# Unused products of 256 bf16 columns between the tiny products of the two compressions, in a two-layer decoder trunk

## The chip, the cores and the metric

The kernel runs on one core of a Trainium2 chip. The metric is the device time of one execution in microseconds (us), from the first to the last instruction and what lies around them. TensorE (PE) has a clock that the chip grants at one of two levels, 2.4 GHz (1.00 in the profile) and 1.2 GHz (0.50).

## The reference, cut to what matters

Two decoder layers on 256 tokens of width 1024. Each layer has one input projection, four parallel mixers (latent attention, a three-branch sparse attention called NSA, a gated linear recurrence, a state-space mixer), an output projection and a feed-forward part; the first layer's is dense, the second's is a mixture of 8 experts. All is float32.

The change lies in NSA's compression: keys and values of 64 dimensions are cut into 15 overlapping blocks of 32 tokens, and each block is multiplied by a weight of 32·64 by 64.

```python
def compress(t, pe, w):
    ch = t.reshape(B, S // CMP_STRIDE, CMP_STRIDE, d)
    blk = jnp.concatenate([ch[:, :-1], ch[:, 1:]], axis=2)
    return ((blk + pe).reshape(B, nc, CMP_LEN * d) @ w).astype(F32)

kc = compress(keys[:, :, 0], cmp_pe[0], w_cmp[0])
vc = compress(vals[:, :, 0], cmp_pe[1], w_cmp[1])
```

with `S` 256, `CMP_STRIDE` 16, `CMP_LEN` 32, `d` 64 and `nc` 15. The results `kc` and `vc` (15 by 64) are the keys and values of the "compressed" attention branch.

## The kernel before, in words

Each engine has its own program, and semaphores tie them together. SyncE (SP) loads weights in units of 1 MB into a ring of seven slots. ScalarE (ACT) copies each unit to a rounded part `w_hi` (L1259 in the mixers, L1281 for the experts), VectorE (DVE) takes the rest as `w_lo` (L1693, L1714), and TensorE makes three one-pass products of each (L450 to L452, and L578, L581 in `by_channel`). These large products fill the feed-forward parts and the input and output projections.

A mixer stage of a layer is written out by hand as TensorE's order: the input projections, then a loop over eight attention jobs `AJ` (MLA, selected, window, compressed; two token blocks each, n = 0 to 7). In step n TensorE does `scores(n)` (a bias product of 512 bf16 columns, L671, that writes the mask, and q·k products, L679), `products(n-2)` (probabilities by values, L713), and `turn_probs(n-1)` (transposes of probabilities, which are products with the identity matrix, L694). Between them stand the other mixers' small products, in this order:

- n = 1: `scores(1)`, `compressed_keys`, `turn_probs(0)`;
- n = 2: `scores(2)`, `products(0)`, `turn_probs(1)`, `compressed_values`;
- n = 3: `scores(3)`, `products(1)`, `turn_probs(2)`, `lru_square` (L800);
- n = 4: `scores(4)`, `products(2)`, `turn_probs(3)`, `ssd_sums` (L754 to L769);
- n = 5 to 7: the same three of each job, `ssd_cb` (L779), `ssd_products` (L789, L792), and the first part of the output projection.

`compressed_keys` (L723) is 32 float32 products that accumulate in one PSUM bank: 64 rows of the array, 64 columns of weights, 15 moving columns each. `compressed_values` (L731) is 32 with 64 rows, 15 columns of weights and 64 moving columns. The trace records each float32 product twice ("x64" for 32), each record with a weight load of its own.

PSUM has eight banks in two pools of four. `bank(0)` hands out the next bank of pool 0 and makes TensorE wait until the reader of its last contents (ACT's exponentials at L1431, DVE's sum at L1924, DVE's copies `kcT` at L1997 and `vc` at L2005) has taken them; `give` says which engine reads it next.

During this stage DVE also runs the recurrence's scan and the state-space mixer's convolutions (L1988 to L1992, L1792, L1795), and ACT the activations that follow (L1474, L1475). The transposes of the normed residual are at L430.

Of the kernel before, what the change touches and what calls it, by code (L numbers as in the profile page):

```python
# [23 lines left out]
P = 128  # L24
# [16 lines left out]
def trunk(nc, x, positions, norm_mix, w_in, mla_q_norm, mla_w_uq, mla_kv_norm, mla_w_ukv, nsa_cmp_pe,  # L41
# [33 lines left out]
    with ctx:  # L75
        def sb(name, shape, dt=F32):
            return ctx.enter_context(nc.sbuf_tensor(name, shape, dt))
# [10 lines left out]
        ident_b = sb("ident_b", [P, P], BF16)  # L88
        cbias = sb("cbias", [P, 2 * P], BF16)
# [299 lines left out]
        def _(pe):  # L389
# [3 lines left out]
            def claim(k):  # L393

                if free_after[k] is not None:
                    pe.wait_ge(*free_after[k])

            def bank(pool):

                k = 4 * pool + used_banks[pool] % 4  # L400
                used_banks[pool] += 1
                claim(k)
                return banks[k]
# [8 lines left out]
            def give(mm, who, b):  # L412

                given[who] += 1
                s = (for_dve, for_act)[who]
                mm.then_inc(s, 1)
                taken(who, b, s, given[who])
# [21 lines left out]
            b = bank(0)  # L439
# [96 lines left out]
            for l in range(L):  # L536
# [162 lines left out]
                def products(n):  # L699
# [15 lines left out]
                    give(mm, 0, b)  # L715
                    mark["pv", l, n] = gave[0]

                def compressed_keys():

                    pe.wait_ge(cin_ready, l + 1)  # L720
                    b = bank(0)
                    for j in range(CLEN):
                        mm = pe.matmul(b[0:HD, 0:NC], w_cmp[0:HD, j, :], cin[0:HD, j, :], start=(j == 0),  # L723
                                       stop=(j == CLEN - 1))
                    give(mm, 0, b)

                def compressed_values():

                    b = bank(0)
                    for j in range(CLEN):  # L730
                        mm = pe.matmul(b[0:NC, 0:HD], cin[HD:P, j, :], w_cmp[HD:P, j, :], start=(j == 0),  # L731
                                       stop=(j == CLEN - 1))
                    give(mm, 0, b)
                    mark["cmp", l] = gave[0]
# [112 lines left out]
                for n in range(1, len(AJ)):  # L847
                    scores(n)
                    if n >= 2:
                        products(n - 2)  # L850
                    if n == 1:
                        compressed_keys()
                    turn_probs(n - 1, 0 if n == 7 else 1)
                    if n == 2:
                        compressed_values()
                    if n == 3:
                        lru_square()
                    if n == 4:
                        ssd_sums()
                    if n == 5:  # L860
                        ssd_cb()
                    if n == 6:
                        ssd_products()
                    if n == 7:
                        turn_output(0)
                        project_output(0)
# [1414 lines left out]
```

## Time and profile before

| what | value |
|---|---|
| runs of the kernel | 1625.79, 1629.19, 1631.63 us; median 1629.19 us |
| profiled execution, its own time | 1629.23 us |
| its span in the profile | 1627.4 us |
| mean granted clock of TensorE | 0.951 |
| PE busy | 1546.0 us, 95% of the span |
| DVE busy | 1229.1 us, 76% |
| ACT busy | 1017.4 us, 63% |
| chain of work that ended last | PE 93%, DVE 3%, issue 2%, ACT 1% |

The profiled execution's time is 1.8 us over its span. "Busy" counts the time in which at least one instruction of the engine is under way. A start time of a row is in us from the span's start; the time that a group of PE instructions holds the engine is best read as the distance to the start of the next one, since the recorded duration of a product includes its way through the array. Layer 0's mixer stage ends near 181 us, layer 1's runs from about 440 to 611 us.

### The profile page before, as it was taken

How to read it: one execution, taken by the hardware profiler on the slowest of the kernel's cores; microseconds unless marked ns; L12 is line 12 of the kernel's file. 1: busy time of each engine (PE TensorE's matmuls, PEld its weight loads, DVE VectorE, ACT ScalarE, POOL GpSimd, SP SyncE). 2: the span in 40 equal slices, each digit the busy share in tenths (PEclk: the TensorE clock that was granted, in tenths of full speed). 3: DMA queues.
4: the chain of work that ended last, by engine and by line, in shares of the span. 5: the costliest groups of instructions: out<-in, count | busy, mean ns of one | idle time of the engine just before them, and what ended most of it. 6: DMA issues, size and time to landing. Idle time of an engine off the chain costs nothing.

```text
span 1627.4 us, 20283 instructions
## 1 busy us (share of the span) xinstructions
PE 1546.0 (95%) x7476; PEld 1292.2 (79%) x7476; DVE 1229.1 (76%) x1150; ACT 1017.4 (63%) x941; POOL 81.8 (5%) x110
## 2 busy tenths in 40 slices
PE   7998799999799984999999999999999999999996
PEld 6887688888689864888888888888888888888884
DVE  6747544444567455888989988988988988988985
ACT  5645343444345522778778778778778778777763
POOL 2100000000000001000000000000000000000000
PEclk9968999999898685999999999999999999999998
DMA  9521555555330052999999999999999999999991
GB/s 288 136 61 60 205 187 198 184 181 192 103 118 1 27 181 78 358 395 358 376 394 356 382 393 352 388 393 344 395 394 343 394 396 342 393 397 352 394 397 43
DMA packets 189878, 444.67 MB, mean 273 GB/s; under 512 B 9633, under 2 KB 15918, under 8 KB 189822
## 3 DMA queue, kind: packets, MB, share of 16 engines
q1 hardware_dynamic: 185214, 427.82, 71.6%
q0 software_dynamic: 4608, 16.10, 3.9%
q8 instruction: 35, 0.57, 0.1%
q14 instruction: 21, 0.17, 0.0%
HBM read 436.03 MB, written 7.86 MB: 273 GB/s over the span
## 4 chain that ended last, share of the span: by engine, by line
PE 93%; DVE 3%; issue 2%; ACT 1%; DMA 0%; POOL 0%; SPq 0%; ACTq 0%; DVEq 0%; POOLq 0%
PE bank L451 25%; PE bank L452 25%; PE bank L450 25%; PE bank L578 3%; PE bank L713 2%; PE bank L505 2%; PE bank L679 2%; PE bank L581 1%; PE bank L694 1%; PE bank L731 1%; PE bank L723 1%; DVE hT L1669 1%; PE bank L915 0%; PE bank L430 0%; DVE w_lo L1693 0%
## 5 line engine op out<-in xcount | busy, mean ns | idle before, releaser
L1714 DVE TENSOR_TENSOR w_lo<-ring,w_hi 128x2048 fp32r<-128x2048 f32 x375 | 853.4, 2290 | 193.3 <-ACT w_hi L1281 192.6
L1281 ACT ACTIVATE w_hi<-ring 128x2048 fp32r<-128x2048 f32 x375 | 716.1, 1915 | 221.6 <-PE bank L450 221.5
L451 PE MATMUL bank<-w_hi,xT_hi 128*128 128x512 f32 x896 | 354.4, 396 | 5.8 <-ACT w_hi L1281 5.8
L452 PE MATMUL bank<-w_hi,xT_lo 128*128 128x512 f32 x896 | 350.4, 391 | 0.0
L450 PE MATMUL bank<-w_lo,xT_hi 128*128 128x512 f32 x896 | 240.4, 390 | 0.0
L451 PE MATMUL bank<-w_hi,hidT_hi 128*128 128x512 f32 x560 | 220.5, 394 | 1.6 <-DVE hidT_lo L1721 1.6
L452 PE MATMUL bank<-w_hi,hidT_lo 128*128 128x512 f32 x560 | 218.3, 390 | 0.0
L451 PEld LDWEIGHTS bank<-w_hi,xT_hi 128*128 128x128 f32 x896 | 168.8, 188 | 40.1 <-ACT w_hi L1281 6.2
L450 PEld LDWEIGHTS bank<-w_lo,xT_hi 128*128 128x128 f32 x896 | 168.7, 188 | 35.7
L452 PEld LDWEIGHTS bank<-w_hi,xT_lo 128*128 128x128 f32 x896 | 169.0, 189 | 33.9
L451 PE MATMUL bank<-w_hi,hT_hi 128*128 128x512 f32 (+2 forms) x384 | 150.3, 395 | 7.9 <-DVE hT_lo L1955 4.5
L450 PE MATMUL bank<-w_lo,hidT_hi 128*128 128x512 f32 x560 | 147.8, 389 | 0.0
L452 PE MATMUL bank<-w_hi,hT_lo 128*128 128x512 f32 (+2 forms) x384 | 147.7, 388 | 0.0
L451 PEld LDWEIGHTS bank<-w_hi,hidT_hi 128*128 128x128 f32 x560 | 105.2, 188 | 23.1 <-DVE hidT_lo L1721 1.8
L450 PEld LDWEIGHTS bank<-w_lo,hidT_hi 128*128 128x128 f32 x560 | 105.1, 188 | 22.2
L452 PEld LDWEIGHTS bank<-w_hi,hidT_lo 128*128 128x128 f32 x560 | 105.2, 188 | 21.3
L1287 ACT ACTIVATE hidT_hi<-bank 128x512 fp32r<-128x512 f32 x70 | 41.2, 599 | 105.0 <-PE bank L505 105.0
L451 PEld LDWEIGHTS bank<-w_hi,hT_hi 128*128 128x128 f32 x384 | 74.6, 194 | 22.8 <-DVE hT_lo L1955 5.0
L450 PE MATMUL bank<-w_lo,hT_hi 128*128 128x512 f32 (+2 forms) x384 | 91.7, 380 | 0.0
L1693 DVE TENSOR_TENSOR w_lo<-ring,w_hi 128x2048 fp32r<-128x2048 f32 (+1 forms) x31 | 70.5, 2282 | 26.3 <-ACT w_hi L1259 25.8
L452 PEld LDWEIGHTS bank<-w_hi,hT_lo 128*128 128x128 f32 x384 | 74.4, 194 | 13.7
L450 PEld LDWEIGHTS bank<-w_lo,hT_hi 128*128 128x128 f32 x384 | 70.2, 188 | 13.6
(344 smaller groups left out, 1380.8 us busy)
## 6 DMA issues: line engine op xcount, KB each, us to landing
ring<-in_moe_w_gate_dram SPq DMA_DIRECT2D x112, 1024.0 KB, 10.0
ring<-in_moe_w_up_dram SPq DMA_DIRECT2D x112, 1024.0 KB, 9.4
ring<-in_moe_w_down_dram SPq DMA_DIRECT2D x112, 1024.0 KB, 9.5
ring<-in_ffn_w_gate_dram SPq DMA_DIRECT2D x14, 1024.0 KB, 5.1
ring<-in_ffn_w_up_dram SPq DMA_DIRECT2D x14, 1024.0 KB, 5.1
ring<-in_ffn_w_down_dram SPq DMA_DIRECT2D x14, 1024.0 KB, 4.8
ring<-in_w_in_dram SPq DMA_DIRECT2D x12, 1024.0 KB, 5.3
ring<-in_w_out_dram SPq DMA_DIRECT2D x8, 1024.0 KB, 5.0
```

What stands on the lines that cost most here:

```text
L450: return pe.matmul(o, x_hi, w, start=False, stop=stop)
L451: pe.matmul(o, x_hi, w, start=start, stop=False)
L452: return pe.matmul(o, x_lo, w, start=False, stop=False)
L505: mm = pe.transpose(banks[2 + v][:, f * P:(f + 1) * P], hid[:, v, f * P:(f + 1) * P], ident[:, :])
L578: mm = pe.matmul(o, wk, hT_hi[:, 4 * h + k, :], start=start and not low, stop=stop and low)
L581: pe.matmul(o, wk, hT_lo[:, 4 * h + k, :], start=False, stop=False)
L679: mm = pe.matmul(b[:, i * nk:(i + 1) * nk], q, k, start=False, stop=(i == per - 1))
L713: mm = pe.matmul(b[:, h * HD:(h + 1) * HD], probT[0:rows, n % 2, i * P:(i + 1) * P], v, start=(kb == 0), stop=(kb == nb - 1))
L1281: act.activation(w_hi[:, (base + at) % SPLIT, :], ring[:, i, :], ACT.Copy).then_inc(hi_ready, 1)
L1287: act.activation(hidT_hi[:, v, :], banks[2 + v][:, :], ACT.Copy).then_inc(hidT_hi_ready, 1)
L1693: dve.tensor_tensor(dst[:, :, 0:n], slot_k(p)[:, :, 0:n], hi[:, :, 0:n], ALU.subtract)\
L1714: dve.tensor_tensor(w_lo[:, v, :], ring[:, (base + at) % RING, :], w_hi[:, v, :].bitcast(F32), ALU.subtract).then_inc(lo_ready, 1)
```

## The change

A helper `stay_warm` issues one product of the 128 x 128 bf16 identity with the 256 bf16 columns of `cbias` (a mask constant) into a spare PSUM bank whose contents nobody reads. Before every second product of both compressions it is called, so 16 times in `compressed_keys` and 16 times in `compressed_values`, in both layers: 64 such products in all. The spare bank is taken from pool 0 with `bank(0)` and never given to a reader.

```diff
+                def stay_warm(b):
+
+                    pe.matmul(b[:, 0:2 * P], ident_b[:, :], cbias[:, :], start=True, stop=True)
+
                 def compressed_keys():
 
                     pe.wait_ge(cin_ready, l + 1)
                     b = bank(0)
+                    spare = bank(0)
                     for j in range(CLEN):
+                        if j % 2 == 0:
+                            stay_warm(spare)
                         mm = pe.matmul(b[0:HD, 0:NC], w_cmp[0:HD, j, :], cin[0:HD, j, :], start=(j == 0),
                                        stop=(j == CLEN - 1))
                     give(mm, 0, b)
@@ -727,7 +734,10 @@
                 def compressed_values():
 
                     b = bank(0)
+                    spare = bank(0)
                     for j in range(CLEN):
+                        if j % 2 == 0:
+                            stay_warm(spare)
                         mm = pe.matmul(b[0:NC, 0:HD], cin[HD:P, j, :], w_cmp[HD:P, j, :], start=(j == 0),
                                        stop=(j == CLEN - 1))
                     give(mm, 0, b)
```

## Rows read from the trace of the kernel before

**Rows 1.** The page's 40 slices of the span: TensorE's granted clock, in tenths.

```profile
PEclk9968999999898685999999999999999999999998
```

**Rows 2.** Stretches from:to in us: length, busy us (xcount) by engine, granted clock, DMA share, GB/s.

```profile
89.64:91.88 2.24, 2.24 (x40) 2.24 (x39) 2.07 (x4) 1.41 (x7) 0.00 (x0) 1.00 0.00 0
91.88:119.20 27.32, 27.32 (x155) 23.18 (x154) 12.54 (x29) 11.56 (x29) 3.43 (x4) 0.50 0.30 60
...
139.70:146.50 6.80, 6.30 (x28) 5.74 (x28) 5.82 (x11) 2.00 (x10) 0.00 (x0) 0.50 0.27 73
...
518.54:556.09 37.55, 37.55 (x184) 32.30 (x184) 17.52 (x41) 17.83 (x42) 0.00 (x0) 0.50 0.09 29
```

**Rows 3.** Timeline of PE in layer 0: start us, busy us, line, tiles, shape, count.

```profile
87.37 0.39 PE L671 MATMUL bank<-cbias,ident_b 128*128 128x512 bf16 x1
87.60 1.03 PE L679 MATMUL bank<-work 96*128 96x256 f32 x4
...
89.64 5.17 PE L723 MATMUL bank<-ring,w_cmp 64*64 64x15 f32 x64
94.74 1.11 PE L694 MATMUL bank<-ident,ring 128*128 128x128 f32 x4
...
101.81 7.00 PE L731 MATMUL bank<-w_cmp,ring 64*15 64x64 f32 x64
108.75 0.61 PE L671 MATMUL bank<-cbias,ident_b 128*128 128x512 bf16 x1
```

**Rows 4.** Timeline of PE in layer 0, behind the return to the full clock.

```profile
119.53 0.38 PE L671 MATMUL bank<-cbias,ident_b 128*128 128x512 bf16 x1
119.84 1.16 PE L679 MATMUL bank<-work 64*128 64x128 f32 x8
120.92 1.10 PE L713 MATMUL bank<-work,ring 128*128 128x64 f32 x8
121.86 1.05 PE L694 MATMUL bank<-ident,ring 128*128 128x128 f32 x8
122.75 0.60 PE L754 MATMUL bank<-ident,work 128*128 128x128 f32 x4
...
126.84 1.13 PE L679 MATMUL bank<-work 64*128 64x256 f32 x4
127.90 0.39 PE L671 MATMUL bank<-cbias,ident_b 128*128 128x512 bf16 x1
```

**Rows 5.** Timeline of PE in layer 1, the same stage.

```profile
514.68 3.90 PE L723 MATMUL bank<-ring,w_cmp 64*64 64x15 f32 x64
518.52 1.11 PE L694 MATMUL bank<-ident,ring 128*128 128x128 f32 x4
...
541.93 1.91 PE L800 MATMUL bank<-hn,ones 128*128 128x256 f32 x4
543.64 0.63 PE L671 MATMUL bank<-cbias,ident_b 128*128 128x512 bf16 x1
...
549.67 1.06 PE L754 MATMUL bank<-ident,work 128*128 128x128 f32 x4
```

**Rows 6.** Waits of PE from 86 to 150 us: us in total, times, longest.

```profile
PE bank L694 <- issue: 0.5, 1, 0.5
```

**Rows 7.** Timeline of DVE and of ACT in layer 0.

```profile
97.27 0.17 DVE L1997 COPY kcT<-bank 64x15 f32<-64x15 f32 x1
```

```profile
106.16 0.61 ACT L1475 ACTIVATE work<-work 128x512 f32<-128x512 f32 x1
```

**Rows 8.** Behind the mixer stage: transposes on PE, and the stretch after them.

```profile
183.82 1.74 PE L430 MATMUL bank<-ident,hn 128*128 128x128 f32 x8 [2.45 <-DVE hn L1660]
185.95 1.80 PE L430 MATMUL bank<-ident,hn 128*128 128x128 f32 x8 [0.40 <-DVE hn L1660]
```

```profile
183.80:187.50 3.70, 3.29 (x16) 2.90 (x16) 1.47 (x3) 2.09 (x4) 0.81 (x2) 0.54 0.00 0
187.50:190.90 3.40, 0.26 (x2) 0.01 (x1) 3.30 (x6) 2.51 (x5) 0.00 (x0) 0.99 0.01 2
```

## The prediction

> **What bounds the kernel now.** The first view is the page: the chain that ended last is 93% PE, and PE is busy 95% of the span. What shortens PE's own stream where nobody else is late shortens the kernel. The second is the clock by slices [rows 1]: it is 9 tenths nearly everywhere but drops to 6 to 8 tenths in a few slices, among them the third (81 to 122 us) and the thirteenth to fifteenth (488 to 610 us), where the mixers run. The third is the stretches [rows 2]: in layer 0 the clock falls to 1.2 GHz at 91.88 us and stays there for 27.32 us; in layer 1 it falls at 518.54 and stays for 37.55 us. PE is busy without a break in both (27.32 of 27.32, 37.55 of 37.55), and its waits over 86 to 150 us add up to 0.5 us [rows 6]. So the engine is not starved there; it does dense work at half rate, and it alone is the path. The fourth view is the timeline [rows 3, 5]: what PE did before each fall is the block of 32 key products of 15 moving columns. In layer 0 it had run 2.24 us of it, in layer 1 all 3.84 us. Before that block the clock was 1.00. After the fall it does not come back through the other attention work, though the same kinds of work at full clock keep it later on (119.5 to 139.7 us).
>
> **The change part by part.** It removes nothing. It adds 16 unused products to each compression of each layer, 64 in all, and one claimed bank to each.
>
> *If the clock stays at 2.4 GHz, the old work gets shorter.* I price every piece between the end of the key block and `ssd_sums` at full clock, by the distance from start to start. From rows 4: a bias product 0.31 (119.53 to 119.84), eight score records of 128 columns 1.08, eight L713 records 0.94, eight transposes 0.89 (so four 0.445), and four score records of 256 columns 1.06 (126.84 to 127.90). `lru_square` has no row fully at 2.4 GHz; at 1.2 it takes 1.71 (541.93 to 543.64 [rows 5]), half is 0.855. The values' 64 records are also seen at 1.2 GHz alone, 6.94 us (101.81 to 108.75 [rows 3]). Half, 3.47, is the lower bound, 6.94 the upper; the key block's 64 records at 2.4 GHz take 3.84 (514.68 to 518.52), and being as many loads and products it is the nearest row, so I take 3.84.
> In order: turn_probs(0) 0.445, scores(2) 1.39, products(0) 0.94, turn_probs(1) 0.89, values 3.84, scores(3) 2 x 1.37 = 2.74, products(1) 1.88, turn_probs(2) 0.445, lru_square 0.855, scores(4) 1.39, products(2) 0.94, turn_probs(3) 0.89. Sum 16.65 us.
> Layer 0 takes 28.01 us for this (94.74 to 122.75 [rows 3, 4]): 11.36 saved. Its key block takes 5.10 (89.64 to 94.74) against 3.84: 1.26 more. Together 12.62.
> Layer 1 takes 31.15 us (518.52 to 549.67 [rows 5]): 14.50 saved. Its `ssd_sums` then runs at half clock until 556.09, 6.42 us, of which half, 3.21, is saved. Together 17.71. Both layers: 30.3 us.
>
> *The unused products themselves.* No row shows one of 256 columns. The bf16 product of 512 columns holds PE 0.23 us in a full stream (87.37 to 87.60 [rows 3]), so its half is 0.115. Below: a weight load of the next tiny product can hide behind it, and a tiny record is 0.06 (3.84 / 64), which leaves 0.06. Above: the same bias product takes 0.31 where the kind of product changes around it, which is 0.08 more, so 0.20. I take 0.12, since the tiny records around it are bound by their loads and part of the switch is hidden. 64 x 0.12 = 7.7 us; bounds 3.8 and 12.8.
>
> *The spare bank.* `bank(0)` makes PE wait for the bank's last reader. In the key block it is the bank of scores(0), whose exponentials are over before the block begins. In the value block it is the same bank again, which no reader was given since. Every later claim in pool 0 then falls on the bank two further on: scores(2) on that of scores(1), values on that of the keys (`kcT`, copied at 97.27 [rows 7]), and from lru_square on each claim again meets the bank of the same earlier job as now. No wait; below nothing is excluded, as nothing is taken away, and above it is some tenths. If one is late it is DVE's `kcT`, because DVE reaches it by its own chain of convolutions; the key block with its products ends at 89.64 + 3.84 + 1.9 = 95.4, the values start at 95.4 + 3.67 = 99.1, 1.6 us behind the copy.
>
> *Other engines at the faster pace.* The cover for everything above is that DVE and ACT keep up. DVE is free of its convolutions at 97.6, and scores(2) now ends at 97.2, so that sum is 0.4 late with nobody behind it until products(2). ACT's L1475 ends at 106.8 [rows 7], and lru_square is reached at 99.1 + 5.76 + 2.74 + 1.88 + 0.445 = 109.9: 3 us of slack. These two follow from work that does not depend on PE's pace. Weight transfers use 0.30 and 0.09 of the DMA engines in the two stretches [rows 2], and those of the later units are released by DVE and ACT steps that move forward with PE. SP's and POOL's queues get nothing new. I price this at 0, up to 2 us if the slack is misjudged.
>
> The sum: 30.3 - 7.7 = 22.6 us off the profiled execution's own 1629.23 us, which is the median of the runs (1629.19): **1606.6 us**. With the bounds of the product's cost it is 1602.7 to 1611.7, and the values' price can add 0.7 off or, far less likely, more on.
>
> **A rule against the change.** PE was busy for all of both stretches, and the clock fell nonetheless [rows 2]. The Trainium skill, TensorE: Matmul & The Clock Gate, section Why this matters for your kernels, says that drops come from PE-idle gaps between bursts of matmuls; taken alone that says there is no gap here to fill, and the products would only be a cost; its outcome is rival B below. The rows speak against it, as the clock fell with no gap at all.
>
> **The rivals.**
> *B, the clock falls in the blocks as before (slower).* Each pair of tiny products is four records at 0.06, 0.24 us, against one unused product of about 0.12 us: the block is still mostly tiny work. If the clock falls about where it does now, everything behind it stays as it is and the unused products come on top: per layer 8 at 0.12 and 24 at the price of the slow clock. That is half of the bias product's 0.54 to 0.57 there, or some 0.25. 8 x 0.12 + 24 x 0.25 = 7.0 us, twice 14: 1643 us. It decides in the key block, the leaner of the two. For it: nothing in the trace shows such a mixture. Against it: scores on 64 rows and products of 64 columns keep 1.00 from 119.5 to 135.9 without a single dense block.
> *C, the clock is held in both blocks and falls behind the values.* There, transposes and small products stand with nothing between them. Then layer 0 gains 1.26, 7.07 - 3.67 = 3.40 up to the values and 3.10 in them, layer 1 the last two: 14.3 - 7.7 = 6.6, so 1622.6 us. The rows speak for the opposite: 16 transposes, and nothing else, ran from 183.82 to 187.7, and the clock rose from 0.5 to 1.00 during them [rows 8]. The Trainium skill, TensorE: Matmul & The Clock Gate, section Part 4: PE-mode transpose, states that a transpose does not count as PE-busy in the same way; by that rule C would be likely. By the trace it is not.
> *D, the clock is held in one layer only.* Where the fall lands differs between the layers now (2.24 and at least 3.84 us into the same block), so chance plays a part. Layer 1 alone: 17.7 - 3.8 - 7.0 = 6.9 off, 1622; layer 0 alone: 12.6 - 3.8 - 7.0 = 1.8 off, 1627.
>
> **How the numbers follow.** Forecast 0.70, B 0.10, C 0.10, D 0.10. Two of the forecast's uncertainties are left: the later half-clock stretches of 6.80 us (139.70, and one like it in layer 1 [rows 2]) can shift by a few us, each worth up to 3.4 us, and runs of one kernel spread by 5.8 us. So the forecast's own range is 1600 to 1613. Reaching to C and to the better case of D gives **1600 to 1623** with 0.84 inside it. About 0.3%, 4.9 us, is what can be told from no change. Faster by more: forecast, C and half of D, 0.84, rounded to 0.83. Within: the other half of D and a B softened by a clock that comes back sooner, 0.06. Slower: the rest of B, with its 14 us, 0.11.
>
> **What would show it.** Right: the granted clock reads 1.00 from the key block to about 137 us (layer 0) and about 555 us (layer 1); the key block and the value block take some 5.8 us each; from the key block to `ssd_sums` PE needs 16.65 + 3.84 + 3.8 = 24.3 us instead of 33.1 and 35.0; the mean clock rises from 0.951 to about 0.97; PE's waits in the stage stay under 1 us. Wrong: a fall inside the key block (B), a fall behind the values with the blocks at full clock (C), idle time of PE at L679, L713 or L694 that DVE or ACT releases (misjudged cover), or blocks longer than 6.5 us at full clock (mis-sized product).

## The result, and the profile after

The change makes the kernel slower: 1646.02 us median (1644.32 to 1650.57, four runs) against 1630.03 us for the kernel before, a ratio of 1.0107 with a 95% interval of 1.0078 to 1.0135. Forecast was 1606.6 us, range 1600 to 1623. The profiled execution took 1645.25 us (span 1643.4), 16.0 more than the one of before.

The page's slices of the granted clock after the change, in tenths, beside [rows 1]:

```profile
PEclk9988899999898686899999999999999999999998
```

The third slice is better than before (8 for 6) and the sixteenth too (6 for 5), but the fifth and the seventeenth are 8 now where they were 9, and the fourteenth, in layer 1's mixers, is 6 as before. The mean clock is 0.952 against 0.951: nothing was won on the whole, and the products came on top.

Stretches of the changed kernel (from:to, length, busy by engine, granted clock, DMA share, GB/s), beside [rows 2]:

```profile
90.17:95.79 5.62, 5.62 (x52) 4.00 (x50) 5.17 (x9) 1.98 (x9) 0.00 (x0) 1.00 0.00 0
95.85:109.36 13.51, 13.51 (x69) 10.34 (x68) 5.84 (x16) 4.66 (x13) 0.00 (x0) 0.50 0.01 2
109.40:143.60 34.20, 34.20 (x265) 27.36 (x265) 20.01 (x46) 23.76 (x60) 4.40 (x6) 1.00 0.35 79
...
518.45:522.40 3.95, 3.95 (x37) 2.80 (x35) 3.61 (x6) 1.98 (x9) 0.00 (x0) 1.00 0.02 6
522.45:563.36 40.91, 40.91 (x193) 27.34 (x193) 11.55 (x29) 12.62 (x27) 0.00 (x0) 0.50 0.05 16
563.40:583.80 20.40, 20.40 (x161) 18.46 (x160) 16.44 (x35) 15.95 (x45) 0.95 (x2) 1.00 0.05 20
```

The clock falls inside the key block of both layers, 5.6 us into it in layer 0 and 4.0 us into it in layer 1 (before: 2.2 us into it, and at its end). It comes back after 13.5 us in layer 0, inside the value block, and only after 40.9 us in layer 1 (before: 27.3 and 37.6).

The timeline of PE in the changed kernel: one group of the key block at the full clock, one at half, the work behind, and groups of the value block. L720 is the unused product, L730 the keys, L741 the values.

```profile
90.71 0.28 PE L720 MATMUL bank<-cbias,ident_b 128*128 128x256 bf16 x1
90.92 0.40 PE L730 MATMUL bank<-ring,w_cmp 64*64 64x15 f32 x4
91.26 0.28 PE L720 MATMUL bank<-cbias,ident_b 128*128 128x256 bf16 x1
...
99.86 0.40 PE L720 MATMUL bank<-cbias,ident_b 128*128 128x256 bf16 x1
100.19 0.61 PE L730 MATMUL bank<-ring,w_cmp 64*64 64x15 f32 x4
100.72 1.11 PE L694 MATMUL bank<-ident,ring 128*128 128x128 f32 x4
...
107.66 0.42 PE L720 MATMUL bank<-cbias,ident_b 128*128 128x256 bf16 x1
...
112.10 0.28 PE L720 MATMUL bank<-cbias,ident_b 128*128 128x256 bf16 x1
112.32 0.39 PE L741 MATMUL bank<-w_cmp,ring 64*15 64x64 f32 x4
112.64 0.28 PE L720 MATMUL bank<-cbias,ident_b 128*128 128x256 bf16 x1
...
116.95 0.39 PE L671 MATMUL bank<-cbias,ident_b 128*128 128x512 bf16 x1
...
126.07 0.60 PE L764 MATMUL bank<-ident,work 128*128 128x128 f32 x4
```

A group of one unused product and four tiny records takes 0.55 us at the full clock (90.71 to 91.26), where four tiny records alone take 0.24. So an unused product adds **0.31 us, not 0.12**. At half clock a group takes about 0.87 us (99.86 to 100.72). Four tiny records alone take about 0.43 there: 64 of the value block take 6.94 [rows 3]. So the product adds 0.44. In the value block at the full clock it is 0.54 (112.10 to 112.64).

Where the time went in us, stage by stage, from the start times of both traces:

| stretch | layer 0 before | after | layer 1 before | after |
|---|---|---|---|---|
| key block | 5.10 | 10.55 | 3.84 | 11.50 |
| turn_probs(0) to the values | 7.07 | 6.94 | 7.07 | 6.94 |
| value block | 6.94 | 9.29 | 6.94 | 13.79 |
| scores(3) to `ssd_sums` | 14.00 | 9.12 | 17.14 | 15.07 |
| `ssd_sums` | 3.78 | 3.78 | 6.86 | 3.78 |
| sum of differences | | +2.8 | | +9.2 |

The two blocks cost 7.8 us more in layer 0 and 14.5 in layer 1; the clock that comes back gives 4.9 back in layer 0 and 5.2 in layer 1. Between the blocks another 0.3 comes back. Together that is 12.0 of the 16.0 us. The other 4 lie in stages that the change doesn't touch (0.5 before the first key block, 2.0 between and behind the two stretches up to the last products, 1.4 at the end), which is within the 5.8 us by which runs of one kernel differ.

### The profile page after: what moved, and what is told of

The parts are those of the page before. It is cut to its first block, busy times and chain, and to the rows that moved or that the text cites. A ratio compares the mean times of both kernels' runs of the same rounds, so it can differ in the third digit from the quotient of the medians.

```text
span 1643.4 us, 20413 instructions
## 1 busy us (share of the span) xinstructions
PE 1560.0 (95%) x7540; PEld 1289.9 (78%) x7540; DVE 1229.3 (75%) x1150; ACT 1017.5 (62%) x941; POOL 81.9 (5%) x110
## 4 chain that ended last, share of the span: by engine, by line
PE 92%; DVE 4%; issue 2%; ACT 1%; POOL 1%; DMA 0%; POOLq 0%; ACTq 0%; DVEq 0%
PE bank L451 25%; PE bank L452 25%; PE bank L450 25%; PE bank L578 2%; PE bank L505 2%; PE bank L713 2%; PE bank L679 1%; PE bank L581 1%; PE bank L720 1%; PE bank L741 1%; PE bank L730 1%; PE bank L694 1%; DVE hT L1679 1%; PE bank L925 0%; PE bank L430 0%
```

## The experiments

Each is written against the changed kernel. "Before" medians on the same chips were 1630.3 to 1631.5 us.

### e1: the same 64 products, but together in the middle of each block

```diff
                     for j in range(CLEN):
-                        if j % 2 == 0:
-                            stay_warm(spare)
+                        if j == CLEN // 2:
+                            for _ in range(16):
+                                stay_warm(spare)
```

(in both blocks)

> The same 64 unused products, but the 16 of each block stand together in its middle instead of before every second tiny product. Theory S (each unused product between tiny ones pays for two changes of the kind of product, about 0.2 us, in which nothing streams; so the block is long and thin and the clock falls): one pair of changes per block is left, a block takes 3.84 + 16 x 0.115 + 0.2 = 5.9 us at full clock, the granted clock stays 1.00 from the key block to about 137 us and in layer 1 likewise; time about 1630.0 - 30.3 + 8.2 = 1608 us. Rival H (the tiny products pull the clock down whatever stands between them, the arrangement does not matter): the clock falls in the key block again and the time stays at 1640 to 1650 us.

Measured: 1617.56 us median (1615.04 to 1623.72), ratio 0.9928 with an interval of 0.9901 to 0.9954. PE in layer 0:

```profile
89.92 2.03 PE L731 MATMUL bank<-ring,w_cmp 64*64 64x15 f32 x32
91.88 1.92 PE L720 MATMUL bank<-cbias,ident_b 128*128 128x256 bf16 x16
93.73 2.03 PE L731 MATMUL bank<-ring,w_cmp 64*64 64x15 f32 x32
95.70 0.66 PE L694 MATMUL bank<-ident,ring 128*128 128x128 f32 x4
...
114.24 0.60 PE L766 MATMUL bank<-ident,work 128*128 128x128 f32 x4
```

and its stretches in both layers:

```profile
95.70:133.00 37.30, 37.30 (x316) 32.45 (x314) 26.96 (x60) 28.21 (x72) 4.38 (x6) 1.00 0.32 73
507.98:515.40 7.42, 7.42 (x93) 6.68 (x93) 6.93 (x13) 2.82 (x10) 0.00 (x0) 1.00 0.02 3
515.45:525.60 10.15, 10.15 (x64) 8.65 (x63) 5.39 (x14) 6.16 (x14) 0.00 (x0) 0.50 0.01 2
```

Sixteen unused products in a row take 1.85 us (91.88 to 93.73), 0.116 each, which is what the prediction worked out for one in a full stream. The key block takes 5.78 us instead of 10.55. In layer 0 the clock holds throughout, and the way from the key block to `ssd_sums` is 24.32 us (89.92 to 114.24). In layer 1 it holds in the block but falls 1.6 us behind it, at 515.4, for 10.2 us. So the number and kind of the products is the same as in the change, and the arrangement alone is worth 28 us. Rival H falls. Layer 1's loss of the clock behind the block explains half of the 10 us by which the time lies above the expectation: from the key block to `ssd_sums` it took 29.12 us (507.98 to 537.10), 4.8 more than layer 0.

### e2: as e1, in the key block only

```diff
-                    spare = bank(0)
                     for j in range(CLEN):
-                        if j % 2 == 0:
-                            stay_warm(spare)
                         mm = pe.matmul(b[0:NC, 0:HD], cin[HD:P, j, :], w_cmp[HD:P, j, :], start=(j == 0),
```

(and e1's edit in `compressed_keys`)

> As e1, but with the 16 products in the key block only; the value block is as in the kernel before. Theory S: the value block, with 64 moving columns in each product, holds the full clock by itself once it begins at it, and the time is about 1630.0 - 30.3 + 4.1 = 1604 us. Rival V (the value block loses the clock when nothing stands in it): the clock is 1.00 up to the value block and falls inside or behind it; the gain is then only the one before the values, 1.3 + 3.4 in layer 0 and 3.4 in layer 1, less 4.1: about 1626 us.

Measured: 1619.23 us median (1617.29 to 1629.63), ratio 0.995, interval 0.9921 to 0.998. The traced run has both outcomes, one in each layer:

```profile
89.57:129.30 39.73, 39.73 (x367) 34.92 (x366) 30.95 (x69) 30.14 (x80) 4.38 (x6) 1.00 0.30 69
...
511.80:535.50 23.70, 23.70 (x123) 19.29 (x122) 8.29 (x22) 11.74 (x26) 0.00 (x0) 0.50 0.09 26
```

In layer 0 the value block, with nothing in it, holds the full clock, so rival V falls there: no unused product is needed among the values. In layer 1 the clock falls at 511.7, again right behind the key block (which ends at 510.18), this time for 23.9 us. Both falls, of e1 and e2, point to the second half of the key block and the work right behind it as the weak place; e5 tries that.

### e3 and e4: what makes an unused product cost 0.31 us

e3 puts it on 64 rows (`r0`, given by the caller, is 0 in the key block and 64 in the value block), e4 in float32 on 128 rows:

```diff
-                    pe.matmul(b[:, 0:2 * P], ident_b[:, :], cbias[:, :], start=True, stop=True)
+                    pe.matmul(b[:, 0:2 * P], ident_b[r0:r0 + HD, :], cbias[r0:r0 + HD, :], start=True, stop=True)
```

```diff
-                    pe.matmul(b[:, 0:2 * P], ident_b[:, :], cbias[:, :], start=True, stop=True)
+                    pe.matmul(b[:, 0:HD], ident[:, :], ident[:, 0:HD], start=True, stop=True)
```

> The change, with each unused product on 64 rows of the array (the same rows as the tiny products around it) instead of 128, still bf16 and 256 columns. Theory S in the form that the change between a 128-row and a 64-row product is what costs: a group of one unused and four tiny records takes 0.24 + 0.12 = 0.36 us at full clock, against 0.546 now. Rival T (the change between bf16 and float32 is what costs): it stays at 0.52 to 0.55 us. Either way the clock still falls in the key block, so the time stays within 1632 to 1650 us.

> The change, with each unused product in float32 (identity by 64 of its columns, two records of about 0.12 us) on 128 rows. Theory S (rows): the group takes 0.24 + 0.24 + 0.2 = 0.68 us at full clock, since the change of rows is still there. Rival T (type): 0.48 us. The clock falls in the key block in both; time 1640 to 1660 us.

One run each: 1655.28 and 1669.53 us, both above what was expected (1650 and 1660 at most). e3 and then e4, PE at the full clock:

```profile
90.28 0.28 PE L720 MATMUL bank<-cbias,ident_b 64*128 64x256 bf16 x1
90.49 0.40 PE L730 MATMUL bank<-ring,w_cmp 64*64 64x15 f32 x4
90.83 0.28 PE L720 MATMUL bank<-cbias,ident_b 64*128 64x256 bf16 x1
```

```profile
91.30 0.43 PE L720 MATMUL bank<-ident 128*128 128x64 f32 x2
91.66 0.40 PE L730 MATMUL bank<-ring,w_cmp 64*64 64x15 f32 x4
91.99 0.32 PE L720 MATMUL bank<-ident 128*128 128x64 f32 x1
```

The group stays at 0.55 us with equal rows (90.28 to 90.83), so the change of rows is not needed for the cost: the form of theory S written for e3 falls. It takes 0.69 us with equal type (91.30 to 91.99), as S said for e4 (0.68) and not T (0.48), so the type is not it either. In both, the unused product still has 128 columns of weights where the tiny ones have 64.

### e6: the unused product on the same tile as its neighbours

```diff
-                    pe.matmul(b[:, 0:2 * P], ident_b[:, :], cbias[:, :], start=True, stop=True)
+                    n = HD if r0 == 0 else NC
+                    pe.matmul(b[0:n, 0:2 * P], ident_b[r0:r0 + HD, 0:n], cbias[r0:r0 + HD, :], start=True, stop=True)
```

> The change, with each unused product on the same tile of the array as the tiny products around it (64 x 64 in the key block, 64 x 15 in the value block), still bf16 and 256 columns. Theory S (the change of tile, rows or columns, costs about 0.2 us per pair, because the next weights are not loaded ahead): a group of one unused and four tiny records takes about 0.36 us at full clock instead of 0.546. Rival T (the change between bf16 and float32 costs it): still 0.52 to 0.55 us. The clock may fall in both.

One run: 1627.68 us. PE in the key block:

```profile
90.70 0.27 PE L721 MATMUL bank<-cbias,ident_b 64*64 64x256 bf16 x1
90.82 0.35 PE L731 MATMUL bank<-ring,w_cmp 64*64 64x15 f32 x4
91.02 0.27 PE L721 MATMUL bank<-cbias,ident_b 64*64 64x256 bf16 x1
```

0.32 us for a group, 0.08 more than the tiny records alone. The type still changes twice in it, so rival T falls. **What costs is the change of tile**: 0.55 against 0.32, 0.23 us for a pair of changes. By e3 a change of columns is enough; that a change of rows alone costs too is seen only in the scores of the kernel before (below). The weight loads show where the time goes. In the changed kernel (PEld, first fence) the tiny products' first load begins 0.21 us after the unused product (90.71 to 90.92); on the same tile (second fence) the next load begins 0.03 us after the last one:

```profile
90.71 0.10 PEld L720 LDWEIGHTS bank<-cbias,ident_b 128*128 128x128 bf16 x1
90.92 0.30 PEld L730 LDWEIGHTS bank<-ring,w_cmp 64*64 64x64 f32 x4
```

```profile
90.67 0.11 PEld L721 LDWEIGHTS bank<-cbias,ident_b 64*64 64x64 bf16 x1
90.70 0.36 PEld L731 LDWEIGHTS bank<-ring,w_cmp 64*64 64x64 f32 x4
```

The Trainium skill, TensorEngine Tiling (Array Packing), section Key Properties, has this rule: changing the tiling mode drains the engine. The traces agree and give the price of 0.23 us, for which the prediction should have looked.

The clock fell in e6 too, in the key block of layer 0 at 93.8 and of layer 1 at 517.1, 3.4 and 4.1 us into it, and came back in layer 0's value block at 104.1. So taking the changes of tile out of the interleaved block did not hold the clock. But this filler differs from that of the change in a second point, as it uses a quarter of the array; no run has full-size filler between the tiny products without changes of tile.

### e7 and e8: one block of the change at a time

e7 leaves the value block as before, e8 the key block (each takes the three added lines out of the other function).

> The change's unused products in the key block only, between the tiny products as in the change; the value block as in the kernel before. The key block of the changed kernel takes 10.6 us in layer 0 and 11.5 in layer 1, against 5.1 and 3.8 before. Theory S: the block still loses the clock and nothing brings it back sooner than before: 1630.5 + 5.5 + 7.7, about 1643 us. Rival R (the rest of the stage profits from the dense work ahead of it): under 1635 us.

> The change's unused products in the value block only; the key block as before, so the clock falls in it. In the changed kernel the clock came back inside layer 0's value block (109.4 us) and not in layer 1's. Theory S: a value block at half clock takes 13.8 us instead of 6.9, and 9.3 where the clock comes back in it, which then saves some 9 us of what follows; so between 1630.5 - 2 x 6 = 1618 us (both come back) and 1630.5 + 2 x 6.9 = 1644 us (neither); with one of each about 1631 us. Rival R2 (the return in layer 0 had nothing to do with the unused products): 1640 to 1645 us in every run.

e7: 1642.62 us median (1640.34 to 1643.92), ratio 1.006, interval 1.0038 to 1.0082, as theory S had it. The clock falls about 4 us into both key blocks and stays down for 34 us (94.6 to 128.7, 528.1 to 562.2).

e8: 1644.35 us median of ten, ratio 1.0061 with an interval of 1.0034 to 1.0087, but the ten fall into three groups: 1622.23 once; 1632.89, 1633.14, 1633.26; and six from 1644.24 to 1650.34. These are about the three values worked out beforehand for "the clock comes back in both value blocks, in one, in neither" (1618, 1631, 1644). The traced run is the 1622.23, and in it the clock is back in both:

```profile
91.90:101.90 10.00, 10.00 (x57) 8.75 (x56) 7.62 (x18) 3.71 (x14) 0.00 (x0) 0.50 0.00 1
102.10:139.50 37.40, 36.35 (x284) 29.06 (x282) 23.53 (x52) 24.97 (x61) 4.39 (x6) 1.00 0.32 73
518.60:525.20 6.60, 6.60 (x29) 5.37 (x27) 5.83 (x15) 3.18 (x12) 0.00 (x0) 0.50 0.00 0
525.40:562.70 37.30, 36.32 (x284) 29.02 (x282) 23.46 (x51) 24.96 (x61) 0.95 (x2) 1.00 0.09 29
```

So the clock comes back, and then stays at 1.00, in value blocks in which unused products and tiny ones alternate at 0.54 us a group, two changes of tile in each (102.1 to 110.4 in layer 0). Whether a half-clock block is left early differs from run to run of one program. That the other two groups are "one" and "neither" is inferred from their times and from their mean granted clocks: 0.961 in the traced run, 0.954 to 0.955 in the group about 1633, 0.944 to 0.948 in the six.

### e9: four products in the middle instead of sixteen

```diff
-                        if j % 2 == 0:
-                            stay_warm(spare)
+                        if j == CLEN // 2:
+                            for _ in range(4):
+                                stay_warm(spare)
```

(key block; none in the value block)

> As e2, but with 4 unused products in the middle of the key block instead of 16. Theory S (how much dense work stands between the tiny products decides): 4 are too few, the clock falls in or behind the block in both layers as in the kernel before, and 2 x 0.7 us come on top: 1630 to 1634 us, the granted clock at 0.50 for some 27 us or more in each layer. Rival Q (a break of any length in the run of tiny products is enough): the clock holds as with 16, 1602 to 1619 us.

Measured: 1632.18 us median of ten (1628.1 to 1639.57), ratio 1.002, interval 0.9998 to 1.0041. The clock falls at 94.0 and 520.7, for 27.4 and 27.3 us. None of the ten runs is near the 1602 to 1619 us of a clock that holds. Rival Q falls: a break in the run of tiny products isn't enough, the amount counts.

### e10: the claims of the spare bank without the products

```diff
                     for j in range(CLEN):
-                        if j % 2 == 0:
-                            stay_warm(spare)
```

(in both blocks)

> The change without its 64 products: both compressions still claim the spare bank, and every later claim of pool 0 falls two banks further on. Theory S: no claim meets a late reader, so the time is that of the kernel before, within 3 us of 1631. Rival W (the shifted claims wait for DVE or ACT): slower than before by more than 5 us, with PE idle at L671, L723 or L731.

Measured: 1630.36 us median, ratio 0.9997 with an interval of 0.9985 to 1.0009. The shifted banks cost nothing, and PE's waits from 86 to 150 us are 0.5 us as before.

### e5: twelve in the middle of the key block, six behind it

```diff
-                        if j % 2 == 0:
-                            stay_warm(spare)
+                        if j == CLEN // 2:
+                            for _ in range(12):
+                                stay_warm(spare)
...
                     give(mm, 0, b)
+                    for _ in range(6):
+                        stay_warm(spare)
```

(none in the value block)

> The key block alone: 12 unused products (256 columns, as in the change) in its middle and 6 behind its last tiny product, none in the value block. In e1 and e2 layer 1 lost the clock right behind the key block, where its last 16 products of 15 columns and the thin scores follow each other. Theory S: six more dense products at that place, which need no change of tile of their own as transposes of the same tile come next, close it; the block takes 3.84 + 12 x 0.115 + 0.2 and the tail 0.7 us; the clock stays 1.00 in both layers; time 1630.5 - 30.3 + 4.5, about 1605 us. Rival P (where the fall lands is chance that more dense work does not change): layer 1 falls again and the time stays near 1618 us.

Measured: **1608.48 us median** (1606.24 to 1610.41), ratio 0.9853 with an interval of 0.9829 to 0.9876: faster than both kernels, 22.7 us below the kernel before. Both layers keep the clock:

```profile
90.52:131.60 41.08, 41.08 (x379) 36.27 (x379) 32.11 (x69) 30.17 (x80) 4.40 (x6) 1.00 0.28 66
...
145.40:155.50 10.10, 7.09 (x22) 5.77 (x23) 7.70 (x11) 3.05 (x6) 1.83 (x2) 0.50 0.54 172
506.58:548.00 41.42, 41.42 (x381) 36.55 (x380) 32.45 (x69) 30.18 (x80) 0.95 (x2) 1.00 0.08 27
```

and PE's stream in layer 0:

```profile
95.87 0.83 PE L720 MATMUL bank<-cbias,ident_b 128*128 128x256 bf16 x6
96.53 0.60 PE L694 MATMUL bank<-ident,ring 128*128 128x128 f32 x4
...
100.28 3.74 PE L741 MATMUL bank<-w_cmp,ring 64*15 64x64 f32 x64
103.95 0.39 PE L671 MATMUL bank<-cbias,ident_b 128*128 128x512 bf16 x1
...
113.07 0.60 PE L764 MATMUL bank<-ident,work 128*128 128x128 f32 x4
```

From the key block to `ssd_sums` it takes 22.55 us in layer 0 (before 33.11) and in layer 1 the same (before 34.99). The value block alone, at full clock, takes 3.67 us (100.28 to 103.95). The six at the end need no tile change of their own, as transposes on the full array follow: 0.66 us together (95.87 to 96.53), 0.11 each. About 3 us of the expectation are missing. Most lies in the output stages behind: from `ssd_sums` to the next normed transposes it takes 62.3 us in layer 0, against 61.1 before, and 62.6 in layer 1, against 64.2, of which `ssd_sums` alone gave back 3.1. Each holds a half-clock stretch of some 10 us, where the one in that place was 6.8 in layer 0. And the faster PE now waits once in each layer for DVE's masking of the last job's probabilities (L1919), 2.0 and 2.2 us, where it waited 0.5; in layer 0:

```profile
134.19 1.01 PE L694 MATMUL bank<-ident,ring 128*15 128x128 f32 x4 [1.98 <-DVE ring L1919]
```

From `ssd_sums` to these transposes it takes 21.12 us, as long as before (122.75 to 143.88), although the clock held some 1.6 us longer in it: the time won is spent on the wait for DVE.

## Why the prediction was wrong, and where it was right

**The view of what bounds the kernel** was right: the half clock in the two mixers, with PE never idle, is time on the path. e5 takes 22.7 us out of it with products whose results nobody reads.

**The price of the old work at full clock** was right to 0.1 us. The forecast was 16.65 us behind the key block without unused products; e5, with none there, takes 16.54 (96.53 to 113.07). The values were taken at 3.84 and measured 3.67.

**The step that failed is "if the clock stays at 2.4 GHz"**: the forecast took it that a key block with an unused product before every second tiny one keeps the clock, and booked 30.3 us for it. In the changed kernel the clock fell 5.6 and 4.0 us into the two key blocks and stayed down for 13.5 and 40.9 us. The two stretches from the key block to the end of `ssd_sums` became 12.0 us longer together, where the sum had them 22.6 shorter.

**The second step that failed is the price of an unused product**: "I take 0.12, since the tiny records around it are bound by their loads and part of the switch is hidden." It measured 0.31 at full clock and about 0.44 at half, beyond the upper bound of 0.20. At these prices, and the clock that each product had, the 64 cost some 24 us instead of 7.7; the clock then gave back some 12 of the 30.3 (both are estimates from the traces' groups, and their difference is the 12.0). The price alone would not have made the kernel slower: 64 at 0.31 are 20 us, and 30.3 less 20 leaves 10, a time of about 1619 us, inside the forecast's range. The lost clock turned the sign.

The row for the price was in hand: the distance of 0.31 from a 128-row bias product to 64-row scores [rows 4] against 0.23 to 96-row ones [rows 3]. I read 0.08 off one side of one such change. The way back was not read at all, although four score records on 64 rows took 1.06 us [rows 4] where four on 96 rows take 0.86 (87.60 [rows 3] to the next bias product):

```profile
88.46 0.38 PE L671 MATMUL bank<-cbias,ident_b 128*128 128x512 bf16 x1
```

A product between tiny ones pays both sides.

**What makes the clock fall in the key block** is shown as far as the arrangement. All ten key blocks with filler between the tiny products (both layers of the changed kernel, e3, e4, e6 and e7) lost the clock 2.4 to 5.6 us after they began; the six with 12 or 16 in one piece (e1, e2, e5) kept it to their end. e1 against the change is the clean pair: same products, same number. Why the arrangement matters stays open. The block became one of 8.7 us at the full clock (16 x 0.55) instead of 5.8, with 0.23 us of every group going to changes of tile, and that would fit; but e6 lost the clock without these changes, and the value blocks of the changed kernel's layer 0 and of e8 kept it with them. e9 shows that four are too few, e2 and e1 that sixteen in the middle leave the place behind the block to chance (kept in layer 0 and lost in layer 1 of both traces). In e5, with six more there, both layers kept it in the one trace taken; its four runs lie within 4.2 us, all below the fastest of e1 and e2. Whether the place or the total of 18 does it is not separated.

**The rivals.** B was right in its main point and close in its time (1643 for 1646; half of the bias product's 0.54 to 0.57 is 0.28, not 0.25, which would have made it 1644 to 1645). Its mechanism, the clock falling in the key block about where it did, is what layer 1 shows. In layer 0 the clock came back early in the value block, which B did not have, and layer 1's `ssd_sums` was spared the half clock, while each unused product cost more than B took. The two errors of some 10 us offset each other, so B's close number is in part luck. C did not happen: no trace shows the clock lost right behind a value block that had kept it, and the stretches with transposes are part of the 41 us at full clock in e5. The rule by which C was likely (the Trainium skill, TensorE: Matmul & The Clock Gate, section Part 4: PE-mode transpose) finds no support in these traces; they record each transpose as a product with the identity, and no run shows whether that is the mode of which the page speaks. The Trainium skill's rule on idle gaps (the same page, section Why this matters for your kernels) gave the right sign, but not by what it says: with no gap to fill, dense products in the right place are worth 22.7 us here (e5).

**Bank claims** were priced at 0 and are at 0: e10's ratio is 0.9997. **DVE, ACT and queues** were priced at 0 for a faster PE, and the changed kernel hardly tests that, as it is not faster. Its PE waits once in each layer, 1.0 us in layer 0 (against 0.5 in [rows 6]) and 1.5 in layer 1, there for DVE. In e5, where PE is faster, these waits are 2.0 and 2.2 us, both for DVE, so the sign "under 1 us" fails there. They lie behind `ssd_sums`, outside the sum of the forecast. Layer 0 of the changed kernel:

```profile
PE bank L694 <- issue: 1.0, 1, 1.0
```

**The chances** gave B 0.10. "For it: nothing in the trace shows such a mixture" should have weighed more: the forecast needed a mixture that no row showed to behave like its neighbours. The row held against B was no match either: the stretch from 119.5 to 135.9 us has `ssd_sums` in it, 3.78 us of products on the full array.

## What to carry to other kernels

Filler that shall keep TensorE's clock up belongs in one piece and not between products of another tile, where each piece cost 0.31 us instead of 0.116; next to work of its own tile it pays no change of tile on that side. Filler on the tile of its small neighbours was cheaper still (0.08 us), but in e6 it did not hold the clock. When a small product is priced, read the distance from start to start across both changes of tile, into it and out of it. And where a block's outcome differs between two layers or ten runs of the same program, one held trace is not a margin: add dense work at the weak place and measure again.

## What the runs showed of the hardware that was not expected

- A change of tile and back costs 0.23 us at the full clock (e6 against the changed kernel, with the same change of type in both), and the group takes as long with only the columns differing (e3). On the same tile, float32 and bf16 products alternate for 0.08 us per 256-column product (0.32 against 0.24), less than the 0.116 that one of the full array takes in a stream (e1). The next load runs under it (90.67 and 90.70 in e6).
- 96 rows behave here as the full array does: the 512-column bias product of 128 rows takes 0.23 us to the start of 96-row scores [rows 3], and 0.31 to that of 64-row ones [rows 4].
- One program's time can fall into groups some 11 us apart, as e8's do, with nothing different that the runs record but the granted clock. The kernel before does it too, seldom: one of 19 of its runs beside e9 took 1619.74 us at a mean clock of 0.957, the others 1628.6 to 1636.0.
